# Two value matrices through one two-step segment of 2x2-block products, with two mixed pairs more, in an fp32r kernel on one core

## What is computed

```python
h = rms_norm(x, norm_mix[l])
proj = jnp.einsum('btd,dn->btn', h, w_in[l])
q_a, f_a, i_a, g_a, q_b, k_b, v_b, gate_logits = jnp.split(proj, split_pts, axis=-1)
...
y_a = hgrn2_mixer(q_a, f_a, i_a, g_a, lower_bounds[l], hgrn_out_gain[l])
y_b = chunked_relpos_attention(q_b, k_b, v_b, q_gain[l], k_gain[l], rel_bias[l])
```

## Time and profile before

| | us |
|---|---|
| median of 3 runs (lowest, highest) | 2128.66 (2128.63, 2129.75) |
| the profiled execution | 2129.49 |
| its span in the trace | 2127.8 |
| PE busy | 2118.4 |
| DVE busy | 1750.3 |
| ACT busy | 1397.1 |
| POOL busy | 224.8 |

### The profile page before, as it was taken

One profiled execution on the slowest core, in us unless ns is written; L12 is line 12 of the kernel. 1 busy time (PEld: TensorE's weight loads), 2 busy tenths in 40 slices (PEclk: granted clock), 3 DMA queues, 4 the chain that ended last, 5 costly groups with the idle time before them and its releaser, 6 DMA issues.

```text
span 2127.8 us, 30210 instructions
## 1 busy us (share of the span) xinstructions
PE 2118.4 (100%) x10098; PEld 1777.5 (84%) x10098; DVE 1750.3 (82%) x2295; ACT 1397.1 (66%) x1617; POOL 224.8 (11%) x314
## 2 busy tenths in 40 slices
PE   9999999999999999999999999999999999999998
PEld 9988888888888888888888888888888888888887
DVE  5578788675666689899899898988989999998976
ACT  6365455466544677766676667768778777876665
POOL 2021433201000000000000000000000111110000
PEclk9999999999999999999999999999999999999999
DMA  7666555676565689889988788877788888887664
GB/s 261 186 189 208 159 158 153 186 220 173 180 187 186 188 245 252 253 250 252 254 253 244 233 244 234 236 221 219 227 245 239 246 245 246 231 233 229 200 195 140
DMA packets 225344, 462.76 MB, mean 217 GB/s; under 512 B 14712, under 2 KB 14816, under 8 KB 225120
## 3 DMA queue, kind: packets, MB, share of 16 engines
q1 hardware_dynamic: 208464, 402.31, 59.6%
q0 software_dynamic: 15744, 55.65, 14.9%
q10 hardware_dynamic: 1040, 3.55, 0.4%
HBM read 409.01 MB, written 3.16 MB: 194 GB/s over the span
## 4 chain that ended last, share of the span: by engine, by line
PE 99%; DMA 0%; DVE 0%; issue 0%; ACT 0%; DVEq 0%; SPq 0%
PE gp L2149 35%; PE gp L2081 33%; PE mx L2149 14%; PE gp L2172 8%; PE gp L2176 4%; PE mx L2429 1%; PE mx L2313 1%; PE mx L2478 1%; PE mx L2129 0%; DMA x_tok<-x_in 0%; PE mx L2316 0%; PE mx L2310 0%; PE mx L2365 0%; PE mx L2409 0%; PE mx L2324 0%; PE mx L2353 0%
## 5 line engine op out<-in xcount | busy, mean ns | idle before, releaser
L733 ACT ACTIVATE w_hi<-raw 128x1024 fp32r<-128x1024 f32 x759 | 797.7, 1057 | 540.0 <-PE gp L2081 257.2
L1324 DVE TENSOR_TENSOR w_lo<-raw,w_hi 128x1024 fp32r<-128x1024 f32 x663 | 807.8, 1232 | 236.0 <-ACT w_hi L733 223.2
L2081 PE MATMUL gp<-w_hi,a_hi 128*128 128x512 f32 x576 | 229.9, 399 | 0.0
L2149 PE MATMUL gp<-w_hi,a_hi 128*128 128x512 f32 x585 | 228.0, 390 | 0.0
L2149 PE MATMUL gp<-w_lo,a_hi 128*128 128x512 f32 x585 | 227.7, 389 | 0.0
L2149 PE MATMUL gp<-w_hi,a_lo 128*128 128x512 f32 x585 | 227.6, 389 | 0.0
L2081 PE MATMUL gp<-w_lo,a_hi 128*128 128x512 f32 x576 | 224.6, 390 | 0.0
L2081 PE MATMUL gp<-w_hi,a_lo 128*128 128x512 f32 x576 | 224.2, 389 | 0.0
L681 POOL DMA_DIRECT2D low<-raw x96 | 81.2, 846 | 1228.2 <-ACT low L740 1228.2
L1567 DVE TENSOR_TENSOR t_lo<-t_sum,t_hi 128x1536 fp32r<-128x1536 f32 x102 | 178.9, 1754 | 10.6 <-ACT t_hi L869 7.5
L869 ACT ACTIVATE t_hi<-t_sum 128x1536 fp32r<-128x1536 f32 x102 | 150.8, 1479 | 5.2 <-PE gp L2149 5.2
(11 more groups left out here) (439 smaller groups left out, 4322.1 us busy)
## 6 DMA issues: line engine op xcount, KB each, us to landing
raw<-a_w_in_in SPq DMA_DIRECT2D x192, 512.0 KB, 5.1
raw<-w_ffn_in_in SPq DMA_DIRECT2D x176, 512.0 KB, 5.3
raw<-w_in_in SPq DMA_DIRECT2D x175, 512.0 KB, 3.7
low<-raw POOLq DMA_DIRECT2D x96, 512.0 KB, 6.6
raw<-w_ffn_out_in SPq DMA_DIRECT2D x88, 512.0 KB, 5.7
raw<-a_w_out_in SPq DMA_DIRECT2D x64, 512.0 KB, 4.6
raw<-w_out_in SPq DMA_DIRECT2D x32, 512.0 KB, 4.2
raw<-w_proj_a_in SPq DMA_DIRECT2D x16, 512.0 KB, 4.0
```

The lines of the kernel that those rows point to most:

```text
L733: act.activation(w_hi[:, place], raw[:, slot], ACT.Copy).then_inc(hi_ready, 1)
L1324: dve.tensor_tensor(w_lo[:, slot], raw[:, slot], w_hi[:, place], ALU.subtract).then_inc(lo_ready, 1)
L2081: ins = pe.matmul(out_, stat, mov, start=start, stop=last and p == 2, skip_group_check=True)
L2149: ins = pe.matmul(out_, stat[sp_], mov[mp], start=start and p == 0, stop=stop and p == 2, skip_group_check=True)
```

## The change

The segments IV and AV become one, VAL, of form "D" with two steps (stride 4096 columns: the first mixer's value, then the second's). In step 0 pairs 4 and 6 are mixed (new), in step 1 pairs 2, 4 and 6 as before. VAL joins the segments with additions by DMA: units 7, 11 and 15 of step 0, units 11 and 15 of step 1. The elementwise work is spread anew (`hgrn_first` in step 0, `hgrn_second` in step 1): the clamp moves from unit 3 to 2, silu from 5 to 6, the two parts of the decays from 7 and 8 to 10 and 12 of step 0, the `Exp` from unit 11 of IV to unit 0 of step 1. In POOL's queue three `add_low` stand ahead of `weigh(0, 0)`, one behind it, one behind the first `head_values`. The last block of QF is evicted ahead of the split for the fourth unit (`ends`).

```diff
+MIXED_VAL = ((4, 6), MIXED)
+ADDED_VAL = ((7, 11, 15), (11, 15))
...
-            Segment(w_in, "N", 1, D, (2 * DM, 2 * DM + NB), 2 * NB, a_op),
-            Segment(w_in, "D", 1, D, (6 * DM, 6 * DM + NB), 2 * NB, a_op),
+            Segment(w_in, "D", 2, D, (2 * DM, 2 * DM + NB), 4 * DM, a_op),
...
-        BY_DMA = (FFN_IN, FFN_OUT, V_IN, UG_IN)
+        BY_DMA = (VAL, FFN_IN, FFN_OUT, V_IN, UG_IN)
...
+            for unit in added_units(VAL, 0):
+                add_low(VAL, 0, unit)
             pool.wait_ge(pre_ready, 2)
             weigh(0, 0)
-            pool.wait_ge(bank_free[1], 1 + block0[IV] // 2 + 1)
+            add_low(VAL, 1, added_units(VAL, 1)[0])
+            pool.wait_ge(val_ready, 2)
             head_values(0, 0)
-            pool.wait_ge(val_ready, 2)
+            add_low(VAL, 1, added_units(VAL, 1)[1])
+            pool.wait_ge(val_ready, 4)
...
-                if j == 11:
+
+            def hgrn_second(i, j):
+                if j == 0:
                     decay_exp(0, 0)
...
-            run(IV, val_out, mid=hgrn_first)
-            double_step(AV, 0, second_out, nothing_between)
+            double_step(VAL, 0, val_out, hgrn_first)
+            double_step(VAL, 1, val_out, hgrn_second)
...
-                return k == OUT and (i, j) == (S[k].steps - 1, S[k].pair - 1)
+                return k in (QF, OUT) and (i, j) == (S[k].steps - 1, S[k].pair - 1)
...
-                if j == 3:
+                if j == 2:
                     dve.tensor_scalar(f_a, f_a, LN_MIN, None, ALU.max).then_inc(pre_ready, 1)
-                if j == 5:
+                if j == 6:
                     dve.tensor_tensor(q_a, q_a, wide[:], ALU.mult).then_inc(pre_ready, 1)
+                if j in (10, 12):
                     dve.wait_ge(consts, 1 + MASKED)
                     dve.wait_ge(ln_ready, 1)
                     dve.wait_ge(pre_ready, 2)
-                if j in (7, 8):
-                    decays(0, 0, j - 7)
+                    decays(0, 0, (j - 10) // 2)
...
-            run(IV, none, mid=hgrn_first)
-            double_step(AV, 0, no_head, no_mid)
-            dve.wait_ge(parts_read, 1)
+            double_step(VAL, 0, no_head, hgrn_first)
+            double_step(VAL, 1, no_head, no_mid)
+            dve.wait_ge(parts_read, 2)
...
-            run(IV)
-            double_step(AV, 0, nothing_between)
-            pe.wait_ge(parts_added, 1)
+            for i in range(S[VAL].steps):
+                double_step(VAL, i, nothing_between)
+            pe.wait_ge(parts_added, S[VAL].steps)
```

More of the change, by code:

```diff
@@ L376, in build @@
         ]
-        QF, IV, AV, G_IN, QK, GATES, PROJ_A, PROJ_B, OUT, FFN_IN, FFN_OUT, V_IN, UG_IN, Y_FIRST, Y_LAST = range(len(S))
+        QF, VAL, G_IN, QK, GATES, PROJ_A, PROJ_B, OUT, FFN_IN, FFN_OUT, V_IN, UG_IN, Y_FIRST, Y_LAST = range(len(S))
         unit0, block0 = [0], [0]
@@ L419, in t_of @@
         def t_of(k):
-            return tx if k == AV else (t_sum, t_hi, t_lo)
+            return tx if k == VAL else (t_sum, t_hi, t_lo)
         def c_of(k):
-            return cx_part if k == AV else c_part
+            return cx_part if k == VAL else c_part
         WIDE = (FFN_IN, V_IN, UG_IN,)
         def mixed(k, i):
-            if k == AV:
-                return MIXED
+            if k == VAL:
+                return MIXED_VAL[i]
             if k == FFN_OUT:
@@ L441, in build @@
         done_steps, done_pairs = {}, {}
-        for k in (AV, FFN_IN, FFN_OUT, V_IN, UG_IN, Y_FIRST):
+        for k in (VAL, FFN_IN, FFN_OUT, V_IN, UG_IN, Y_FIRST):
             done_steps[k] = sum(S[q].steps for q in done_steps)
@@ L507, in raw_use @@
             return i * (16 * S[k].pair // RAW) + 16 * ((unit0[k] + j) // RAW + 1)
-        BY_DMA = (FFN_IN, FFN_OUT, V_IN, UG_IN)
+        BY_DMA = (VAL, FFN_IN, FFN_OUT, V_IN, UG_IN)
         def added_units(k, i):
+            if k == VAL:
+                return ADDED_VAL[i]
             if k == FFN_OUT:
@@ L646, in head_values, with add_low @@
                 pool.tensor_copy(v_head[:], val[:, which, :, bass.ds(h * DH, DH)]).then_inc(v_ready, 1)
+            made = [0]
+            def add_low(k, i, unit):
+                buf = added(k, i, unit)[0]
+                made[0] += 1
+                pool.wait_ge(neg_ready, made[0])
+                pool.dma_start(low[:, buf].bitcast(F32), raw[:, raw_slot(k, i, unit)], accum_op=ALU.add).then_inc(lo_added[buf], 16)
+            for unit in added_units(VAL, 0):
+                add_low(VAL, 0, unit)
             pool.wait_ge(pre_ready, 2)
             weigh(0, 0)
-            pool.wait_ge(bank_free[1], 1 + block0[IV] // 2 + 1)
+            add_low(VAL, 1, added_units(VAL, 1)[0])
+            pool.wait_ge(val_ready, 2)
             head_values(0, 0)
-            pool.wait_ge(val_ready, 2)
+            add_low(VAL, 1, added_units(VAL, 1)[1])
+            pool.wait_ge(val_ready, 4)
             load_gate_rows(pool, 0)
@@ L895, in double_step, with val_out @@
                         mid(i, j)
[L897 to L903, removed]
+            def val_out(i, half):
                 for t, c in enumerate(((0, 3), (2, 1))[half]):
-                    ins = act.activation(val[:, 1, t, half * NB:(half + 1) * NB], cx_part[:, c], ACT.Copy, scale=rx[:, t:t + 1])
+                    ins = act.activation(val[:, i, t, half * NB:(half + 1) * NB], cx_part[:, c], ACT.Copy, scale=rx[:, t:t + 1])
                 own.link(ins)
@@ L2220, in shared_banks @@
                         pe.wait_ge(ws_copied, 1)
-                elif k == AV:
+                elif k == VAL:
                     pe.wait_ge(parts_added, dbl(k, i))
@@ L2243, in mixed_pair @@
                 else:
-                    s1_, s2_, s3_, s4_ = [[x_[:, q] for x_ in ((sx_hi[:, n], sx_lo[:, n]) if k == AV else s_of(u // 2))]
+                    s1_, s2_, s3_, s4_ = [[x_[:, q] for x_ in ((sx_hi[:, MIXED.index(u)], sx_lo[:, MIXED.index(u)]) if k == VAL else s_of(u // 2))]
                                           for q in range(4)]
```

10 lines of the change are left out of this document (1 added, 9 removed).

## The result

| | before | after |
|---|---|---|
| median of 8 runs each, same chip (lowest, highest) | 2128.74 (2128.31, 2130.48) | 2135.03 (2133.77, 2135.49) |
| the profiled execution, its span | 2129.49, 2127.8 | 2134.89, 2132.3 |

The ratio is 1.0029 [1.0020, 1.0038]: the change costs 6 us, where 4.9 were forecast.

A forecast was written before the change was run, and what follows sets the result against it. PE, busy throughout, was taken to bound the kernel. Six fewer matmuls (-1.36) plus waits of 3.0, 0.7, 0.6 and 1.9 gave +4.9 us on 2128.66: 2133.6 us, range 2129.0 to 2138.0.

The forecast's parts named there:

- matmuls taken away: In the merged value stage six fewer PE matmuls than in IV and AV, 0.227 us each: -1.36 us.
- bank 0: At the boundary of steps 0 and 1, PE waits 3.0 us (2.0 to 3.5) because DVE frees the bank late.
- bank 1: One unit into step 1, PE waits 0.7 us more for the second half's bank, freed at 154.6, wanted at 153.95.
- split of unit 7, step 1: DVE, slowed beside POOL's `weigh`, finishes this split 0.6 us late for PE.
- `low` of unit 11, step 1: The DMA addition queued behind POOL's `weigh(0, 0)` lands at 184.9; PE, there at 183.0, waits 1.9 us.
- DVE's 34.2 us against 32.3: Step 0: DVE's work from the second sigmoid's end until bank 0 is free, against the time until PE wants it.
- rival D: DVE isn't late at the boundary of the two steps, so PE doesn't wait: -1.36 to +0.5 us; chance 0.14.
- POOL: In step 1 the 17 `weigh` instructions, alternating with DVE's, take 18 to 19 us instead of 14.1.
- Rival B: Only the boundary waits come; `weigh` stays at 14.1 us and no split is late: +2.3 us, 2131.0; chance 0.25.
- C: In step 1 DVE starves POOL, `weigh` takes 22 us and more, `low` is 6.5 to 8.5 late: about +9.5 us; chance 0.14.
- The clock: A 3 us wait at the boundary lowers PE's clock, losing 2.7 us per unit: 2136 to 2139 us; chance 0.04.
- Nothing for the other four additions: The stage's other DMA additions have copies 8 to 10 us ahead, against landing times of 5.6 to 6.6: no wait.

The follow-up runs named there:

- second trace: The changed kernel run once more, unaltered, for another profile: median 2134.44 us, ratio 1.0027 to the kernel before; profiled execution 2134.69 us.
- first trace: The original profiled execution of the changed kernel, set against the kernel before: 2134.89 us, span 2132.3 us, value stage 5.74 us longer.

## Why the forecast came out as it did

**Right, with its steps.** The sign, the size and the places. The second trace, undisturbed by the clock, carries the sum term by term:

| term | forecast | second trace, as recorded | the same, from matmul to matmul |
|---|---|---|---|
| matmuls taken away | -1.36 | -1.36 | -1.36 |
| bank 0 | 3.0 | 2.71 | 2.98 |
| bank 1 | 0.7 | 0.41 | 0.68 |
| split of unit 7, step 1 | 0.6 | 0.57 | 0.83 |
| `low` of unit 11, step 1 | 1.9 | 1.91 | 2.19 |
| sum | 4.9 | 4.2 | 5.3 |

The last column takes the distance between the starts of the matmuls around a wait, less 0.227 for each matmul; the stage's 5.46 less 5.3 are matmuls at 0.235 instead of 0.227 behind a wait. By it **each stop costs 0.25 to 0.3 us beyond its recorded wait**: 0.16, since the record of a matmul lasts 0.39 where the next would start after 0.227, and 0.11, since the first spacing behind a stop is 0.34. The forecast counted PE's arrival by spacings, so this is the column to set it against: both banks are right to 0.02, the split and `low` are 0.2 and 0.3 short. The four terms aren't four independent costs: together they are how late `low` of unit 11 lands, as the two traces show.

**DVE's 34.2 us against 32.3.** The forecast had the additions start at 146.9 and bank 0 free at 151.15, with QF's end at 105.95. In the second trace, whose stage starts in the same place, they start at 146.59 and PE is let go at 150.91. The arithmetic of the queue was right to 0.3, and rival D is out; the versions with decays moved and with one pair less confirm the cause from two sides.

**POOL.** `weigh` was forecast at 18 to 19 us against 14.1 in the earlier trace rows; it took 19.5 (159.39 to 178.87), and the DMA landed 5.5 us later against the 5.6 of the earlier trace rows. In the first trace the wait was 2.17. Two slips stand in the working and change nothing: 2.77 for two splits beside POOL is set against 2.27, where the record of two alone is 1.22 + 1.13 = 2.35 by the earlier trace rows, which is what its 0.21 each comes from; and its 170.35 contains unit 6, which the sentence leaves out. The taking of turns was right: of the 17 instructions the first two, before DVE had begun, took 0.4 and 0.5, the others 0.9 to 2.0, one for each DVE instruction beside them. Rival B, 14 us as before, is out; so is C, where single instructions should have taken 3 to 8 us. The Trainium skill, SBUF — State Buffer, section "SBUF: two separate sides", calls the shared port pair an exclusive lock for a whole instruction, taken by whoever starts first. The turns in `weigh` and the 1.50 beside the 1.33 agree with it. It doesn't say who comes next when both are ready, and the 8.36 us in which a split got no turn between sixteen POOL instructions show that this can be the same engine each time.

**The clock: mis-sized.** The forecast gave a fall 0.04 and 2.7 us per unit. It was there in the first trace, with 1.54 us over seven matmuls, and took the place of bank 1's 0.7 and nearly all of the split's 0.6. The step that failed is the chance: the rows of before had no wait over 1.3, which says nothing about 3.0, and of eight stops of 1.9 to 2.8 us in the traces of the changed kernel and its variants, at this boundary and in step 1, two were followed by a fall. The Trainium skill, TensorE: Matmul & The Clock Gate, Part 1, has the clock set by how busy the array has been recently. The traces agree so far that every fall in them stands behind a stop; they show no length of stop that decides it.

**"Nothing for the other four additions": wrong by little.** Unit 15 of step 0 waited 0.16 in the first trace (asked for at 138.12, landed some 8 us later) and not at all in the second; with both parts moved unit 11 of step 0 waited 0.43 after a landing of 8.80. The step took the least and the median of the earlier trace rows, 5.6 to 6.6, for additions that had 8 to 10 us to spare, where the row's largest was 10.2.

**The eviction** cost nothing where it stands now, and 0.9 where it stood: both as forecast.

**"No later move".** Between the first trace and that of before the spans differ by 4.5 and the starts of G_IN by 4.7, in the second by 5.3 and 5.5: nothing behind the stage moved by more than 0.2. Stage +5.46 to +5.74, medians +6.1 and +6.3. The profiled execution of before lies 0.8 above its median, those of after within 0.3 of theirs, which is within the scatter of 1 us ahead of the stage. No wait behind the stage differs by more than some tenths.

**Left open.** Why the clock falls in one execution and not in another; and what makes a train out of ready POOL instructions. That no variant beats the kernel before by a measurable amount follows from 1.36 being 0.06%: the best, with both parts moved, gives back 0.66 in the trace and nothing that the medians can tell.

## What to carry to other kernels

Before a change takes work from the engine that bounds, add up the queue of the engine that serves it between two points that are tied to others' work (here: the second sigmoid, and the bank of the next step). Where the sum is over the time, every microsecond over comes back as a wait; here the sum gave the moment to 0.3 us. A transfer issued behind a long run of another engine's work is late by that run; but freeing it can pack the run into a train that starves its neighbour, so look at what the moved instruction used to space out. Count a stop from the start of one matmul to the start of the next, some 0.3 us more than the recorded wait, and land DMA additions by the largest landing time and not by the median.

## What the runs showed of the hardware

- A DVE split of 1.2 us took 8.36 in one trace and 8.80 in another, beside 17 POOL instructions that had been ready behind a DMA issue and began 0.37 to 0.49 apart. The same instructions, let go by PE's semaphore instead, took turns with a split: 1.33.
- TensorE's clock fell to its 1.2 GHz level behind stops of 1.95, 2.30, 3.17 and 3.49 us and not behind eleven others of 1.12 to 2.71, 2.44 and 2.71 among them. It lasted seven to nine matmuls of 512 columns and began at once (2.30, 3.49) or 1.5 us after PE was let go (1.95, 3.17). One kernel showed both.
- A stop of PE costs 0.25 to 0.3 us beyond its record: 2.71 recorded, 2.98 from matmul to matmul, and the next start is 0.34 behind instead of 0.23.
- A DMA addition into `low` landed 4.9 to 8.8 us after its issue in this stage, over the traces of all versions.
